# Latent attention heads: scores from split float32r passes in place of a plain float32 product

## The reference

```python
q = jnp.einsum('bsc,chd->bshd', c_q, w_uq)            # 16 heads, 64 + 32 columns
...
q_rope = apply_rope(q_rope, ...) * ATTN_SCALE
k_rope = apply_rope(k_r, cos, sin)                    # one rotary key for all heads
q_lat = jnp.einsum('bshn,chn->bshc', q_nope, w_uk) * ATTN_SCALE
...
s = einsum('bqhc,bkc->bhqk', ql, c_kv) + einsum('bqhr,bkr->bhqk', qr, k_rope)
p = jax.nn.softmax(s.astype(jnp.float32), axis=-1)
return jnp.einsum('bhqk,bkc->bqhc', p, c_kv)
```

## Time and profile before

| what | value |
|---|---|
| median of 3 runs | 1565.17 us (1562.39 to 1565.42) |
| the profiled execution's own time | 1564.39 us |
| its span | 1562.3 us |
| PE busy | 1523.4 us, 98% |
| DVE busy | 1217.6 us, 78% |
| ACT busy | 877.4 us, 56% |
| POOL busy | 117.2 us, 8% |
| the 16 heads | about 705 to 761 us of the span |

### The profile page before, as it was taken

One profiled execution on the slowest core, in us unless ns is written; L12 is line 12 of the kernel. 1 busy time (PEld: TensorE's weight loads), 2 busy tenths in 40 slices (PEclk: granted clock), 3 DMA queues, 4 the chain that ended last, 5 costly groups with the idle time before them and its releaser, 6 DMA issues.

```text
span 1562.3 us, 19111 instructions
## 1 busy us (share of the span) xinstructions
PE 1523.4 (98%) x7361; PEld 1218.0 (78%) x7361; DVE 1217.6 (78%) x1782; ACT 877.4 (56%) x1349; POOL 117.2 (8%) x180
## 2 busy tenths in 40 slices
PE   7999999999999999999999999999999999999997
PEld 4878876878878887766788887877788888787876
DVE  1898978988868888665585654669888798888996
ACT  2545436544447444377564544655567477777774
POOL 1110020000001000015211000000001000000000
PEclk9999999999999999999999999899999999999999
DMA  9999856988857988333286544445324479989893
GB/s 345 374 378 357 301 202 217 333 301 305 305 178 264 339 285 309 118 109 108 82 310 189 185 147 142 157 152 193 113 81 131 162 258 363 344 316 334 306 344 132
DMA packets 196400, 373.75 MB, mean 239 GB/s; under 512 B 9042, under 2 KB 102672, under 8 KB 196304
## 3 DMA queue, kind: packets, MB, share of 16 engines
q1 hardware_dynamic: 176688, 301.08, 55.8%
q0 software_dynamic: 18928, 69.77, 12.7%
q10 hardware_dynamic: 688, 1.62, 0.3%
HBM read 371.39 MB, written 1.05 MB: 238 GB/s over the span
## 4 chain that ended last, share of the span: by engine, by line
PE 89%; ACT 4%; DVE 4%; POOL 1%; DMA 1%; SPq 1%; issue 1%; DVEq 0%; ACTq 0%
PE banks L524 25%; PE banks L526 25%; PE banks L525 25%; PE banks L1165 1%; ACT arena L807 1%; ACT uh L449 1%; DVE ul L460 1%; PE banks L2409 1%; DMA raw<-in_ffn_w_in 1%; PE banks L3011 1%; PE banks L835 1%; PE banks L981 1%; PE banks L2018 1%; PE banks L1843 1%; PE banks L766 1%
## 5 line engine op out<-in xcount | busy, mean ns | idle before, releaser
L460 DVE TENSOR_TENSOR ul<-raw,uh 128x1024 fp32r<-128x1024 f32 (+2 forms) x548 | 657.1, 1209 | 156.3 <-ACT uh L449 147.2
L449 ACT ACTIVATE uh<-raw 128x1024 fp32r<-128x1024 f32 (+2 forms) x548 | 568.4, 1048 | 346.7 <-PE banks L526 342.4
L524 PE MATMUL banks<-uh,hh 128*128 128x512 f32 (+2 forms) x1296 | 517.4, 399 | 4.2 <-DVE ul L460 1.9
L526 PE MATMUL banks<-uh,hl 128*128 128x512 f32 (+2 forms) x1296 | 503.9, 389 | 0.0
L525 PE MATMUL banks<-ul,hh 128*128 128x512 f32 (+2 forms) x1296 | 503.0, 388 | 0.0
L524 PEld LDWEIGHTS banks<-uh,hh 128*128 128x128 f32 x1296 | 245.5, 189 | 60.3 <-issue 6.1
L526 PEld LDWEIGHTS banks<-uh,hl 128*128 128x128 f32 x1296 | 245.3, 189 | 51.1
L525 PEld LDWEIGHTS banks<-ul,hh 128*128 128x128 f32 x1296 | 245.9, 190 | 45.4 <-issue 0.2
L524 PE MATMUL banks<-uh,bh 128*128 128x512 f32 x512 | 207.3, 405 | 1.0 <-DVE bl L3208 0.9
L526 PE MATMUL banks<-uh,bl 128*128 128x512 f32 x512 | 200.0, 391 | 0.0
L525 PE MATMUL banks<-ul,bh 128*128 128x512 f32 x512 | 199.5, 390 | 0.0
(11 more groups left out here) (402 smaller groups left out, 1267.0 us busy)
## 6 DMA issues: line engine op xcount, KB each, us to landing
raw<-in_ffn_w_in SPq DMA_DIRECT2D x176, 512.0 KB, 6.7
raw<-in_w_up SPq DMA_DIRECT2D x64, 1024.0 KB, 6.5
arena<-in_ada_w POOLq DMA_DIRECT2D x60, 1024.0 KB, 7.4
raw<-in_ffn_w_out SPq DMA_DIRECT2D x44, 1024.0 KB, 5.7
raw<-in_w_down SPq DMA_DIRECT2D x32, 1024.0 KB, 6.2
raw<-in_w_in SPq DMA_DIRECT2D x22, 1024.0 KB, 5.0
raw<-in_ada_w SPq DMA_DIRECT2D x12, 1024.0 KB, 10.5
raw<-in_w_mem_kv SPq DMA_DIRECT2D x4, 1024.0 KB, 6.0
```

Source lines behind the costliest of these rows:

```text
L449: act.e.activation(uh[r][:, 0:w], raw[m % NRAW][:, h * w:(h + 1) * w], AF.Copy).then_inc(act_done, ta.put("hi", u))
L460: dve.e.tensor_tensor(ul[r][:, 0:w], raw[m % NRAW][:, h * w:(h + 1) * w], uh[r][:, 0:w].bitcast(F32), ALU.subtract).then_inc(dve_done, tv. ...
L524: pe.e.matmul(o, a, wh, start=k + j == s0, stop=False)
L526: mm = pe.e.matmul(o, b, wh, start=False, stop=k + j == s1)
```

## The change

ACT's copy of the turned bank now goes to float32r buffers (`qk_high`, the halves of `bh`, which the feed-forward blocks use at other times). DVE gets a new step `low(h)`: the bank minus the high part, into `qk_low` (the halves of `bl`). It stands at the head of each of DVE's turns. The score product is made of three float32r passes of 96 x 128 by 96 x 256, added in the bank: high by high, high by low, low by high (queries first). `one(h)` waits for `low(h)`, and the turned bank is freed by `low(h)` in place of `high(h)`.

```diff
+        qk_high = [flat2(bh[:, 2 * i:2 * i + 2, :]) for i in range(2)]
+        qk_low = [flat2(bl[:, 2 * i:2 * i + 2, :]) for i in range(2)]
+        SCORE_PARTS = [(qk_high, qk_high), (qk_high, qk_low), (qk_low, qk_high)]
...
-                pe.frees(b, act_done, ta, "qk", q, h)
+                pe.frees(b, dve_done, tv, "qk", q, h)
...
-                pe.wait_ge(act_done, ta("qk", q, h))
+                pe.wait_ge(dve_done, tv("qk", q, h))
                 pe.take(b)
                 for t in range(T):
-                    mm = pe.e.matmul(PB[b][:, A.scores(t)], qk[h % 2][0:hd, t * P:(t + 1) * P],
-                                     qk[h % 2][0:hd, S:2 * S], start=True, stop=True)
+                    for n, (a, k) in enumerate(SCORE_PARTS):
+                        mm = pe.e.matmul(PB[b][:, A.scores(t)], a[h % 2][0:hd, t * P:(t + 1) * P],
+                                         k[h % 2][0:hd, S:2 * S], start=(n == 0), stop=(n == 2))
...
-                act.e.activation(qk[h % 2][0:hd, :], PB[QK_BANKS[h % 2]][0:hd, :], AF.Copy).then_inc(
+                act.e.activation(qk_high[h % 2][0:hd, :], PB[QK_BANKS[h % 2]][0:hd, :], AF.Copy).then_inc(
                     act_done, ta.put("qk", q, h))
...
+            def low(h):
+                i = h % 2
+                dve.wait_ge(act_done, ta("qk", q, h))
+                dve.e.tensor_tensor(qk_low[i][0:A.hd, :], PB[QK_BANKS[i]][0:A.hd, :],
+                                    qk_high[i][0:A.hd, :].bitcast(F32), ALU.subtract).then_inc(
+                    dve_done, tv.put("qk", q, h))
...
             for s in range(A.nh + 3):
+                if s < A.nh:
+                    low(s)
                 if s >= 3:
                     one_over(s - 3)
```

## The result

The change is slower: a median of 1576.18 us (1573.31 to 1577.86, 6 runs) against 1564.09 (1562.37 to 1565.42, 6 runs), a ratio of 1.008 with a 95% interval of 1.007 to 1.0091, or +12.1 us. The forecast was 1574 (8.7 us more than before), with its own case ending at 1577.5.

A forecast was written before the change was run, and what follows sets the result against it. A closed ring across engines, with the reciprocal's place in DVE's order, was taken to bound the heads. Start 2.1, six pairs 6.1 and tail 0.5 made +8.7 us, so 1574 us, range 1568 to 1582.

The forecast's parts named there:

- its own case: Whole kernel, forecast without the rivals: range 1571 to 1577.5 us, from the bounds of its terms; chance 0.62.
- The ring: Closed chain through DVE, POOL, PE and ACT in the heads: 6.30 us per two heads against 5.28 before.
- h as above: The head whose reciprocal starts at 730.96 us, from which the steps of the ring were counted.
- start: First heads: low(0) waits for DVE's last query rotation, so one(2) comes 2.1 us later, bounds 1.8 and 2.4.
- six pairs: Heads from one(2) to one(14): 1.02 us more for each of six pairs, 6.1 us.
- tail: Last heads, where output products stand between them: 0 to 1.0 us more, taken as 0.5.
- The price of the passes: PE's scores: six split passes take 0.72 us against 0.87 for a plain pair, a gain of 0.15 a head.
- The 2.4 us "by itself": PE's scores over all heads: 16 x 0.15 us gained if the cheaper passes were the only effect.
- low: DVE's subtraction in each head: 0.64 us, bounds 0.60 and 0.75, standing ahead of the reciprocal.
- Rival A: PE's clock in the heads falls again: one to three more falls add 1.2 to 9.9 us; chance 0.26.
- B: DVE's idle time takes all of low, leaving only PE's gain: 1562.8 us; chance 0.05.
- C: POOL's queue covers the late reciprocals and only the late first head is paid: about 1565 us; chance 0.07.

The follow-up runs named there:

- a: The change with DVE's low(s) moved behind one_over(s-3) instead of ahead of it: 1564.02 us, 1.0013 of the kernel before.
- d: The change with low kept in place but unread, scores being one plain float32 product of the high parts: 1576.77 us, 1.0086 of the kernel before.
- the second: Profile from measuring the unaltered change once more: 1576.25 us, 1.0090 of the kernel before.
- k: The change with five useless products ahead of two(h) at even h and eight ahead of the first scores: 1571.93 us, 1.0064 of the kernel before.
- c: The change without low, scores made of three split passes of the high parts alone: 1561.66 us, 0.9996 of the kernel before.
- j: The change with low(0) ahead of DVE's last rotation and five useless products ahead of two(h) at even h: 1569.94 us, 1.0047 of the kernel before.
- e: The change with five useless PE products ahead of two(h) at even h: 1575.03 us, 1.0082 of the kernel before.
- g: The change with low(s) behind one_over(s-3) and low(0) ahead of DVE's last rotation of queries: 1561.10 us, 0.9992 of the kernel before.
- f: The change with low(0) alone moved ahead of DVE's last rotation of queries: 1576.17 us, 1.0088 of the kernel before.
- i: The kernel before, with DVE's pair_out moved one turn later, behind the next reciprocal: 1562.68 us, 0.9999 of the kernel before.

## Why the prediction was right, and where its sizes were off

- **The bound and the mechanism.** Right. The ring was forecast step by step as 6.30 us and measured as 6.36 to 6.38; a and d show that the place of the reciprocal makes it. One label was wrong: the forecast goes round with "h as above", an odd head, but `three` stands between `one(h+3)` and the next `zero` only for even h. The trace has it so: in the kernel before the ring runs through the odd share (730.96 is the reciprocal of head 7), after the change through the even one (share(2) at 721.47 to share(4) at 727.83). The steps and their sum are not touched by it, the tail is.
- **The total.** By terms, start, six pairs and tail, the heads were forecast 8.7 us longer. The first profile of the change has 3.2 + 7.9 + 2.3 = 13.4, the second 3.2 + 7.1 + 0.8 = 11.0, and k, whose heads have no stretch at 0.50, 2.1 + 4.3 + 1.9 = 8.3. So the sum was close for a full clock, and most of what it lacked is the clock, which it held as a rival. That its own case, up to 1577.5, still took in the measured 1576.2 is in part luck: that room was made by the bounds of other terms.
- **The price of the passes.** Inside the group right: 0.12 us apart. But the first pass after the transposes takes 0.20 and the last is followed by 0.21, so one to three is 0.90 us and not 0.72 (0.41 of two to one, not 0.49, gives a part back). Net that is 0.10 more a ring; low gave 0.03 back, and 0.06 to 0.08 was missing in all. The plain products ahead of `three` take 0.96 (d) and not the 0.87 that was read ahead of `zero`. On the ring lies one score pair in two heads, and it is worth 0.15 us, as c shows (5.28 to 5.13). The 2.4 us "by itself" was not seen: c's heads are 1.4 us shorter and its time 0.5, no more than chance.
- **low.** Forecast 0.64 from its start to the next, measured 0.61, with a median duration of 686 ns over the 16.
- **The start.** Forecast 2.1, measured 3.17 (from first transposes to one(2): 6.10 before, 9.27 after). The wait of the first score is as forecast (2.24 us later against 2.25). The missing part is the clock: passes in the first head start 0.21 apart, at 0.50, and `one(0)` to `one(2)` takes 5.61; at full clock, in j and k, it takes 4.53.
- **The six pairs from one(2) to one(14).** Forecast 6.1, measured 7.9 (32.92 to 40.83): 6 x 1.10 = 6.6 at full clock, as in j, and two falls of 1.1 and 1.3 us, less the fall at 712 that the kernel before had here (1.2 us). PE's wait for share was forecast as about 1 us a pair and is 1.83.
- **The tail.** 0.5 forecast, 2.3 measured (15.78 to 18.10) in the first profile and 0.75 in the second, which has a fall just ahead of it; at full clock it is 1.9 (j, 17.64, and likewise e and k). By that figure it is the term that was most short for its size. I had taken one(14) as the last point of the ring, but the wait falls between the even and the odd head: one(14) to one(15) is 1.86 us before and 3.64 after, and that step stood in no term.
- **Rival A** was given 0.26 as an alternative. It happened beside the forecast and not in its place: about 2 to 5 of the 12 us. The likeness it argued from was borne out. "The new waits are shorter than 1.8 us each" was no reason against it: PE waited 1.2 to 1.8 us a pair and at the end 2.3; in the second profile four waits of 1.8 in a row stood ahead of the one fall, in the first a single one ahead of each of two. The Trainium skill, "TensorE: Matmul & The Clock Gate", section "HAM oscillation — how this bites in real kernels", tells of a loop that waits about 3 to 5 us for a DMA behind each burst of matmuls. The prediction took it as a rule for any such wait, which it does not say; no wait of PE in these heads is longer than 2.3 us, and the clock still fell once to three times in 40 us of the loop, so here the measurement decides.
- **The count of passes.** The Trainium skill, "FP8 and Floating Point Precision", section "TensorE Precision Notes", counts four passes for true float32, and by that estimate the scores would be still cheaper than 0.72; with 0.90 measured it leads away from the number.
- **Rivals B and C** fell with the result. a shows what each had right: DVE's idle time can take low in the loop, and the start alone is paid (1.0013), but only where low stands behind the reciprocal.

## What to carry to other kernels

On an engine that works strictly in order, a new step can cost more than its own 0.69 us: it brings a wait, which is paid by whatever stands behind it. So ask of each instruction behind it whose ring it is on, and put the new step behind the urgent one. Idle time of an engine is cover only if it lies after the place of insertion. And when waits on PE grow, count the low clock as part of the same price, not as an alternative. Work of no use in the gaps bought back 2.5 to 5 us of the heads here; by the medians it was 4 to 6 us, where the start was filled or early too, and nothing that could be told apart where it was not.

## What was not expected of the hardware

The program up to the first transposes of the heads is the same in all these kernels, yet these started between 704.29 us (the change) and 707.55 us (g). The windows of before, then of g, show why: the first stretch at low clock is longer in some executions, and one more comes near 280 us.

```profile
15.00:40.00 25.00, 21.52 (x130) 12.74 (x123) 6.43 (x13) 6.60 (x9) 0.00 (x0) 0.86 1.07 369
255.00:300.00 45.00, 43.12 (x208) 35.23 (x207) 39.98 (x61) 23.89 (x35) 3.01 (x4) 1.00 0.83 290
```

```profile
15.00:40.00 25.00, 20.53 (x121) 12.05 (x113) 6.13 (x11) 6.34 (x9) 0.00 (x0) 0.80 1.07 369
255.00:300.00 45.00, 43.12 (x201) 35.09 (x200) 38.44 (x59) 23.77 (x35) 2.26 (x3) 0.96 0.81 276
```

The same goes for the part behind the heads. Counted from the last `three`, all these executions keep step to within 0.1 us up to about 965 us; then the clock is low for a time that differs from one to the next (in c and k once more near 1250 us), and by the end g is 2.5 us shorter than before and f 1.6 longer. The windows of before, i and g there:

```profile
965.00:1010.00 45.00, 42.35 (x202) 36.65 (x200) 32.26 (x69) 28.89 (x61) 3.60 (x8) 0.85 0.36 119
```

```profile
965.00:1010.00 45.00, 42.65 (x197) 36.83 (x196) 30.62 (x66) 28.65 (x61) 3.19 (x7) 0.81 0.40 128
```

```profile
965.00:1010.00 45.00, 42.13 (x213) 35.83 (x213) 32.17 (x69) 30.38 (x65) 3.87 (x9) 0.92 0.42 134
```

A profiled execution can so differ by 3 us ahead of the place of interest and by 4 behind it, for one and the same code. Inside the heads the falls can differ too, as the two profiles of the change show (68.2 and 65.8 us), while the pairs at full clock repeat to 0.01 us. Distances inside a stage, at one level of the clock, compare kernels better than spans do, and effects of 1 to 2 us to the end need the medians of many runs.
